# A fused two-block kernel on one core: attentions with a deeper order, six weight places, norms split by bank

## The reference

```python
# first block
h = rms_norm(x, norm_mix);  u = h @ w_in                  # 4896 columns
y_a = short_conv(u);  y_n = nsa_mixer(u);  y_g = gated_deltanet(u)
x = x + (sum_r sigmoid(h @ w_gate + b_gate)_r * (y_r @ w_branch[r])) @ w_out
h = rms_norm(x, norm_ffn)
x = x + hier_moe(h)        # 4 groups x 8 = 32 experts, the best group, 2 experts in it, FF 512
# second block: modulate(t, shift, scale) comes from silu(c) @ ada_w
x = x + g1 * mla_mixer(modulate(rmsnorm(x)));   x = x + g2 * swiglu(modulate(rmsnorm(x)))
x = x + g1 * mamba2_mixer(modulate(rmsnorm(x))); x = x + g2 * moe_swiglu(modulate(rmsnorm(x)))
return rmsnorm(x, final_norm)                             # moe_swiglu: 8 experts
```

## Time and profile before

| | us |
|---|---|
| median of 3 runs | 2620.92 |
| lowest and highest | 2620.5, 2622.52 |
| the profiled execution | 2633.1 |
| its span in the trace | 2631.3 |
| PE busy in it | 2230.7 (85%) |
| DVE busy | 1436.3 (55%) |
| ACT busy | 1155.0 (44%) |
| mean granted clock of PE | 0.894 |

### The profile page before, as it was taken

The page is one execution under the profiler, slowest core; times in us unless marked ns, Lnnn a source line. Parts: engine busy times, 40 slices in busy tenths (PEclk is TensorE's granted clock), DMA queues, the critical chain, the costliest instruction groups (busy, mean ns, idle before and its releaser), DMA issues.

```text
span 2631.3 us, 29041 instructions
## 1 busy us (share of the span) xinstructions
PE 2230.7 (85%) x11922; PEld 1662.9 (63%) x11922; DVE 1436.3 (55%) x1992; ACT 1155.0 (44%) x1489; POOL 40.9 (2%) x107
## 2 busy tenths in 40 slices
PE   6888898766677665787799889888999999999997
PEld 6767566552222211455799777667887888878875
DVE  4744435333011000332455576557989988988997
ACT  3432333320000000242344356645777777777775
POOL 0000100000000000000000000000000000000000
PEclk9889898767777788897899889788999999999999
DMA  7451830219999999657344432134989989989994
GB/s 255 167 185 49 281 135 33 96 64 387 409 409 409 409 409 409 248 198 287 112 156 182 160 128 97 64 128 158 343 319 370 336 321 369 338 318 372 337 341 193
DMA packets 267688, 656.66 MB, mean 250 GB/s; under 512 B 13454, under 2 KB 38546, under 8 KB 267544
## 3 DMA queue, kind: packets, MB, share of 16 engines
q1 hardware_dynamic: 266592, 652.90, 67.1%
q10 hardware_dynamic: 952, 1.77, 0.2%
HBM read 653.60 MB, written 1.05 MB: 249 GB/s over the span
## 4 chain that ended last, share of the span: by engine, by line
PE 67%; DMA 16%; DVE 9%; ACT 5%; issue 2%; POOL 0%; ACTq 0%; DVEq 0%; POOLq 0%
PE psum L241 16%; PE psum L242 16%; PE psum L243 16%; PE psum L236 11%; DMA ring<-in_w_expert_up 5%; DMA ring<-in_w_expert_down 5%; DMA ring<-in_w_expert_gate 5%; PE psum L2278 2%; PE psum L1043 2%; DVE w_lo L186 2%; PE psum L835 1%; ACT w_hi L176 1%; PE psum L2300 1%; DVE xbc L841 1%; DMA ring<-in_ada_w 1%
## 5 line engine op out<-in xcount | busy, mean ns | idle before, releaser
L186 DVE TENSOR_TENSOR w_lo<-ring,w_hi 128x1024 fp32r<-128x1024 f32 (+1 forms) x778 | 904.8, 1179 | 404.0 <-ACT w_hi L176 391.0
L176 ACT CAST w_hi<-ring 128x1024 fp32r<-128x1024 f32 (+1 forms) x778 | 785.2, 1015 | 448.5 <-PE psum L243 444.9
L241 PE MATMUL psum<-w_hi,xg_hi 128*128 128x512 f32 (+1 forms) x768 | 293.9, 383 | 1.2 <-ACT xg_lo L1961 1.2
L243 PE MATMUL psum<-w_lo,xg_hi 128*128 128x512 f32 (+1 forms) x768 | 288.8, 376 | 0.0
L242 PE MATMUL psum<-w_hi,xg_lo 128*128 128x512 f32 (+1 forms) x768 | 288.7, 376 | 0.0
L2278 PE MATMUL psum<-ring,hT 128*32 128x512 f32 x1024 | 169.8, 799 | 117.3 <-DMA ring<-in_w_expert_gate 62.7
L2278 PEld LDWEIGHTS psum<-ring,hT 128*32 128x32 f32 x1024 | 32.6, 129 | 248.7 <-DMA ring<-in_w_expert_up 86.6
L241 PEld LDWEIGHTS psum<-w_hi,xg_hi 128*128 128x128 f32 x768 | 144.6, 188 | 30.5 <-issue 1.8
L242 PEld LDWEIGHTS psum<-w_hi,xg_lo 128*128 128x128 f32 x768 | 144.6, 188 | 29.0 <-issue 1.7
L243 PEld LDWEIGHTS psum<-w_lo,xg_hi 128*128 128x128 f32 x768 | 144.4, 188 | 28.5
L2130 DVE TENSOR_TENSOR x<-x,psum 128x1024 f32<-128x1024 f32 x14 | 17.1, 1221 | 244.0 <-PE psum L236 244.0
(11 more groups left out here) (653 smaller groups left out, 3838.0 us busy)
## 6 DMA issues: line engine op xcount, KB each, us to landing
ring<-in_moe_w_gate SPq DMA_DIRECT2D x40, 2048.0 KB, 9.4
ring<-in_moe_w_up SPq DMA_DIRECT2D x40, 2048.0 KB, 10.2
ring<-in_moe_w_down SPq DMA_DIRECT2D x40, 2048.0 KB, 9.2
ring<-in_w_expert_gate SPq DMA_DIRECT2D x32, 2048.0 KB, 16.7
ring<-in_w_expert_up SPq DMA_DIRECT2D x32, 2048.0 KB, 17.1
ring<-in_w_expert_down SPq DMA_DIRECT2D x32, 2048.0 KB, 17.7
ring<-in_ada_w SPq DMA_DIRECT2D x24, 2048.0 KB, 8.3
ring<-in_ssm_w_in SPq DMA_DIRECT2D x10, 2048.0 KB, 8.0
```

What stands on the lines that cost most here:

```text
L176: a.copy(self.buffers(n, src.shape)[0], src).then_inc(*self.hi_made.up())
L186: v.tensor_tensor(lo, src, hi.bitcast(F32), SUB).then_inc(*self.lo_made.up())
L241: p.matmul(o, l[0], r[0], start=start, stop=False)
L243: return p.matmul(o, l[0], r[1], start=False, stop=stop)
```

## The change

1. **Attentions.** PE multiplies the values of job m-1 behind the transposes of job m; before it did those of job m right behind its own transposes. DVE's `finish` comes one step later too. The loops have one more step, in which `beside` isn't called.
2. **Places.** Six of the twelve units of group 0 have buffers of their own: gate 0 and 1 in memory of the NSA mixer (`place_ns`), up 2 and 3 in memory of `w_hi` and `w_lo` (`place_w`), down 0 and 1 in memory of the stage's own tensors (`place_fe`). SP waits for the end of the NSA mixer before the first two and for the last multiplied unit of the output projection before the other four.
3. **Table.** `table_dve` is cut in five pieces of three rounds, one in each of the groups 1 to 5, behind the gather.
4. **Norms.** Of each bank pair DVE turns tiles 0 and 1 and ACT tiles 2 and 3 into `hT`; the high and low halves are made by two tiles, and PE starts on the first four tiles and waits for the others at its fifth (`ready`). The router's logits take tiles 0 to 3 for both token tiles first. The state space mixer's `dt` product waits for `hT` alone.
5. **Weights of the groups.** The reciprocal and two multiplications that weight the gates by the group's probability stand behind the start of the places' count.

The diff, cut to its core:

```diff
@@ Ring @@
+    def add_beside(self, src, tensor, loaded):
+        self.beside.append((src, tensor, loaded))
+        return -len(self.beside)
+    def load_beside(self, e, u):
+        src, tensor, loaded = self.beside[-u - 1]
+        src = src(None)
+        e.dma_start(tensor[:, :].rearrange("p (k n) -> p k n", k=src.shape[1]), src).then_inc(loaded, 16)
@@ memory @@
+    place_w = [sb(f"place_w{n}", [P, UNIT], where=places) for n in range(2)]
+    sb("under_places", [P, 1248], where=mg)
+    place_ns = [sb(f"place_ns{n}", [P, UNIT], where=mg) for n in range(2)]
+    place_fe = [sb(f"place_fe{n}", [P, UNIT], where=fe) for n in range(2)]
+    places = {(0, 0, 0): place_ns[0], (0, 0, 1): place_ns[1], (0, 1, 2): place_w[0], (0, 1, 3): place_w[1], (0, 2, 0): place_fe[0],
+              (0, 2, 1): place_fe[1]}
@@ norm_dve @@
-            for k in range(4):
+            for k in range(2):
...
-        if h is not None:
-            for k4 in (0, 4):
-                v.wait_ge(*st.act.of("h_hi", k4))
-                v.tensor_tensor(h[1][:, k4:k4 + 4, :], hT[:, k4:k4 + 4, :], h[0][:, k4:k4 + 4, :].bitcast(F32),
-                                SUB).then_inc(*st.dve.up("h", k4))
+            if h is not None:
+                for k in ((0, 2) if k4 == 0 else (2, 0)):
+                    two = slice(k4 + k, k4 + k + 2)
+                    v.wait_ge(*st.act.of("h_hi", k4 + k))
+                    v.tensor_tensor(h[1][:, two, :], hT[:, two, :], h[0][:, two, :].bitcast(F32), SUB).then_inc(*st.dve.up("h", k4))
@@ ACT's part of a norm @@
-    def norm_split_act(a, st, h):
+    def norm_turned_act(a, st, h, gain, shift):
         for k4 in (0, 4):
-            a.wait_ge(*st.dve.of("hT", k4))
-            a.copy(h[0][:, k4:k4 + 4, :], hT[:, k4:k4 + 4, :]).then_inc(*st.act.up("h_hi", k4))
+            a.wait_ge(*st.pe.of("hT", k4))
+            ps = banks.of(st.name, "hT", k4)
+            for k in (2, 3):
+                a.activation(hT[:, k4 + k, :], ps[:, k * T:(k + 1) * T], ACT.Identity if shift else ACT.Copy, scale=gain(k4 + k),
+                             bias=shift(k4 + k) if shift else 0.0).then_inc(*st.act.up("hT", k4))
+            banks.empty(st.act, st.name, "hT", k4)
+            if h is not None:
+                for k in ((0, 2) if k4 == 0 else (2, 0)):
+                    a.wait_ge(*(st.act if k else st.dve).of("hT", k4))
+                    a.copy(h[0][:, k4 + k:k4 + k + 2, :], hT[:, k4 + k:k4 + k + 2, :]).then_inc(*st.act.up("h_hi", k4 + k))
@@ by_feature_pe; by_token_pe likewise @@
+                if ready and f == 0 and k == 4:
+                    p.wait_ge(*ready)
@@ attention_pe @@
-        for n in range(len(jobs) + AHEAD):
+        for n in range(len(jobs) + AHEAD + 1):
...
-            if beside:
+            if beside and n < len(jobs) + AHEAD:
                 beside(p, n)
             m = n - AHEAD
-            if m >= 0:
+            if 0 <= m < len(jobs):
...
                 ins.then_inc(*st.pe.up("shown", m))
+            m -= 1
+            if m >= 0:
+                job = jobs[m]
                 p.wait_ge(*st.act.of("pT", m))
                 ps = banks.take(p, st.name, "out", m)
@@ attention_dve @@
-            m = n - AHEAD
+            m = n - AHEAD - 1
@@ logits @@
+    def logits_pe(p, st, w):
+        ps = banks.take(p, st.name, "logits")
+        for k4 in (0, 4):
+            for signal in (st.dve, st.act):
+                p.wait_ge(*signal.of("hT", k4))
+            for t in range(NT):
+                for k in range(k4, k4 + 4):
+                    ins = p.matmul(ps[:, t * 512:t * 512 + w.shape[2]], hT[:, k, t * P:(t + 1) * P], w[:, k, :],
+                                   start=k == 0, stop=k == KD - 1)
@@ groups_dve @@
-                table_dve(v, S["moe1"], moe1)
...
+            if 1 <= i < 6:
+                table_dve(v, S["moe1"], moe1, 3 * (i - 1), MOST_OVER_GROUPED if i == 5 else 3 * i)
@@ mix_act @@
         split.make_hi(a, PARTS)
...
-        norm_split_act(a, st, h_mix)
+        norm_turned_act(a, st, h_mix, lambda k: col("norm_mix", k), None)
@@ sync @@
         start_sync(s)
+        ring.load(s, run1.units[0, 0, 2])
+        finished(s, S["nsa"])
+        for n in range(2):
+            ring.load_beside(s, run1.units[0, 0, n])
+        ring.load(s, run1.units[0, 1, 1] + 1)
+        s.wait_ge(*split.multiplied(unit["out", 1]))
+        for g, n in ((1, 2), (1, 3), (2, 0), (2, 1)):
+            ring.load_beside(s, run1.units[0, g, n])
         ring.load(s, run1.units[31 // GROUP, 2, 3] + 1)
```

More of the change, by code:

```diff
@@ L110, in __init__ @@
         self.units, self.emptied, self.now, self.next = [], None, {}, 0
+        self.beside = []
     def restart(self):
@@ L131, in loaded @@
     def loaded(self, u):
+        if u < 0:
+            return self.beside[-u - 1][2], 16
         return self.slot_loaded[u % SLOTS], 16 * (u // SLOTS + 1)
     def slot(self, u):
+        if u < 0:
+            return self.beside[-u - 1][1][:, :]
         return self.tensor[:, u % SLOTS, :]
     def empty(self, signal, u):
-        self.now[u] = signal.last()
+        if u >= 0:
+            self.now[u] = signal.last()
 class Split:
@@ L804, in by_token_pe @@
             kn = hi.shape[1]
+            if ready and k0 == 4:
+                p.wait_ge(*ready)
             for half, out_ in enumerate(outs):
@@ L951, in mix_pe @@
         norm_pe(p, st, xn_mix)
-        for k4 in (0, 4):
-            p.wait_ge(*st.dve.of("h", k4))
+        p.wait_ge(*st.dve.of("h", 0))
         for n in range(3):
-            by_feature_pe(p, unit["conv", n], h_mix)
+            by_feature_pe(p, unit["conv", n], h_mix, ready=None if n else st.dve.of("h", 4))
         for n in range(4):
@@ L2436, in moe1_pe @@
         norm_pe(p, st, xn_ffn)
-        p.wait_ge(*st.dve.of("hT", 4))
-        ps = banks.take(p, "moe1", "logits")
-        for t in range(NT):
-            ins = product(p, ps[:, t * 512:t * 512 + 36], [(hT[:, k, t * P:(t + 1) * P], w_rout[:, k, 0:36]) for k in range(KD)])
-        ins.then_inc(*st.pe.up("logits"))
+        logits_pe(p, st, w_rout[:, :, 0:36])
         places_pe(p, st, moe1)
@@ L2563, in mla_pe @@
             ps = banks.take(p, "unit", u)
-            by_token_pe(p, u, h_mla, [[ps[:, t * 512:t * 512 + w] for t in range(NT)]])
+            by_token_pe(p, u, h_mla, [[ps[:, t * 512:t * 512 + w] for t in range(NT)]], ready=None if n else st.dve.of("h", 4))
         modulation_pe(p, st, spread0)
@@ L2845, in ffn_pe @@
         norm_pe(p, st, xn_ff)
-        for k4 in (0, 4):
-            p.wait_ge(*st.dve.of("h", k4))
+        p.wait_ge(*st.dve.of("h", 0))
         for c, nf in enumerate(ff_chunks):
             for g in range(2):
-                by_feature_pe(p, unit["ff", g, c], h_ff, nf)
+                by_feature_pe(p, unit["ff", g, c], h_ff, nf, ready=None if c or g else st.dve.of("h", 4))
         pairs = [banks.take(p, "ff_down", half) for half in range(2)]
@@ L2972, in ssm_pe @@
         ins.then_inc(*e.up("dt"))
-        by_feature_pe(p, unit["ssm", "b", 0], h_ssm)
+        p.wait_ge(*st.dve.of("h", 0))
+        by_feature_pe(p, unit["ssm", "b", 0], h_ssm, ready=st.dve.of("h", 4))
         modulation_pe(p, st, spread1)
@@ L3356, in moe2_pe @@
         norm_pe(p, st, xn_moe)
-        p.wait_ge(*st.dve.of("hT", 4))
-        ps = banks.take(p, "moe2", "logits")
-        for t in range(NT):
-            ins = product(p, ps[:, t * 512:t * 512 + 8], [(hT[:, k, t * P:(t + 1) * P], w_rout[:, k, 36:44]) for k in range(KD)])
-        ins.then_inc(*st.pe.up("logits"))
+        logits_pe(p, st, w_rout[:, :, 36:44])
         for t in range(NT):
```

61 lines of the change are left out of this document (38 added, 23 removed).

## The result

| | us | ratio to before |
|---|---|---|
| kernel before, median | 2620.8 | |
| changed kernel, median of 4 (2527.8 to 2540.1) | 2536.0 | 0.9671 [0.9645, 0.9697] |
| changed kernel, a later set, median of 5 (2538.0 to 2542.8) | 2542.1 | 0.9689 [0.9675, 0.9702] |
| profiled execution of the changed kernel | span 2526.1, run 2527.8 | |

It is 85 us faster in the first set and 79 in the later one, where 66 were forecast; the first lies at the lower end of the range. Executions of one kernel differ: by 12 us here, and the kernel before lay between 2616.2 and 2633.1 in all of its runs. The profiled execution of the changed kernel is the fastest of its four, while the profiled one of before was 12 us above its median. The two traces are therefore 105 us apart and the medians 85.

What follows compares the result with a forecast made beforehand. No single bound: the chain is 67% PE and 16% DMA, so each part was weighed where it lies. The terms -25.7 - 11 - 13.4 - 12.0 - 4 = -66.1 took the median 2620.92 to 2555 us, range 2536 to 2578.

Steps and rivals of the forecast that it cites:

- Places, -25.7: First experts' groups: six units leave the DMA traffic, 30.7 us, less 3.5 for a later first slot and 1.5 empty queue.
- NSA attention, -11: NSA attention: most of PE's 17.7 us of waits for ACT's copies of the turned probabilities go, saving 11 us.
- rival D: Both attentions: waits move to bank pairs or DVE's scaling, some 15 of 24.4 us come back; 2570 us, chance 0.12.
- MLA attention, -13.4: MLA attention: six waits of about 1.07 us go (6.4), and PE ends 7.0 us earlier at the last job.
- Norms, -12.0: Six norms: DVE and ACT share the tiles, so PE starts earlier in five; first norm 1.0 us longer; sum -12.0.
- The three small steps: First experts' norm: three small DVE steps leave the path, saving 0.75 us.
- Clock, -4: NSA attention: denser work regains a quarter of the clock loss in two low stretches, 4 us, bounds 0 and 14.
- Rival B: Both attentions: the clock stays at 2.4 GHz, 10 us more gained; 2545 us, chance 0.16.
- A: Whole kernel: the sum of the terms holds; 2555 us, own range 2542 to 2568, chance 0.55.
- C: First experts' group 0 doesn't keep up, by half clock or an empty queue; places give -16, 2565 us, chance 0.14.
- E: Both attentions: transposes and products side by side bring PE to half clock; slower, 2674 us, chance 0.03.
- The sum: Whole kernel: the five terms together give -66.1 us, from the median of 2620.92 to 2555.

Runs made afterwards that it cites:

- e3_norms: The kernel before with the norms by banks and the moved weights of the groups alone: 2604.0 us, ratio 0.9936.
- e8_norm_filler: The changed kernel with 20 to 24 unread identity products on PE ahead of the transposes of four norms: 2533.1 us, ratio 0.9662.
- after_again: The changed kernel as it is, measured once more in a later set: 2542.1 us, ratio 0.9689.

## Why the prediction came out too high

**Places, -25.7.** Right: 25.8 in the stage, 23.8 alone. The 5.12 us for a unit, the first slot 3.5 us later and the ten units in time held; the 1.5 us of an empty queue did not occur. The trace keeps 409 GB/s, so the figure of 358 GB/s in the Trainium skill, "DMA: Bandwidth & Descriptors", section "Where 436 GB/s comes from", doesn't bind here. The table in pieces cost nothing, as counted. Whole it takes 10.6 us of the stage, less than half of the 22 us of small steps that the prediction put there. In nine traces with the six places and the table in pieces the stage takes 454.0 to 455.0 us, whatever the clock.

**NSA attention, -11.** Right as a term for the waits: 11.5. The two waits for banks came, but longer (5.4 with 2.8 foreseen). Of the 15 us of rival D, at 0.12, these 5.4 are all that came.

**MLA attention, -13.4.** Too much for its mechanism: 9.8. The term is more than PE waited for the copies there at all, 12.3: its 7.0 for the end stand against waits of 4.81 and 1.10. The end of the earlier trace rows is shorter as meant, the last transposes lie in the wait and both products follow each other, but that wait is still 2.5 us, because ACT's four high halves of the output weights stand ahead of the copy as before.

**Norms, -12.0.** The five norms were forecast at -1.75, -3.2, -3.1, -2.2 and -2.0 and gave -2.0, -3.2, -3.1, -2.2 and -2.3; the first norm +1.0 and gave +0.7. The three small steps, forecast at -0.75, gave -0.9 (logits to the selection 14.47 and, in e3_norms, 13.55). The heading says -14, but the sum goes by -12.0. Beside them 3.2 us in the last experts were not foreseen. Part alone: 16.5.

**Clock, -4.** This is the step that failed. It was read from two stretches of the NSA attention alone, a quarter of their 14.5 us, nothing for MLA and nothing behind the norms. Removing the waits raised the clock in both attentions and was worth about 12 us for the order alone (33.1 less 21.3 of waits) and 14 to 21 in the changed kernel (35.6 to 42.4 less 21.3). Rival B named the mechanism and had 0.16, but was priced from the same two stretches, 10 us more than A, so that even it ended at 2545. The reason given against it, the first experts at 0.77 with PE busy two thirds of the time, was no argument: that stage is full of gaps (one of 2 to 3 us for each unit), and its clock rose from 0.78 to 0.88 in the trace after without any gain: e8_norm_filler has 0.78 in it and takes only 1.0 us more, since DMA sets its end. The rule of the Trainium skill, "TensorE: Matmul & The Clock Gate", section "What's actually happening", that activity releases the throttle, would have given the better number; fillers that change nothing but PE's activity show it in this kernel, though the stretch from 390.9 us on, at 0.51 with PE busy throughout, fits it less well.

**Rivals C and E** did not come: no wait for DMA in group 0, and no half clock through the attentions.

**The sum.** Alone, the parts save 23.8, 33.1 and 16.5 us, 73.4 together, with 25.7, 28.4 (order and clock) and 12.0 forecast. So 7.3 of what was missed lies in the order and the norms, where the clock gave 8 more than its 4 and the MLA term 3.6 less than was counted. The other 6 to 11 us, up to 79.4 or 84.8, are seen only with the parts together; what makes them stays open.

A second fault lies under the sum: the terms were taken from one trace, 12 us above the median, in which the NSA attention was at the slow one of its two values (150.0 against 143.4).

## What to carry to other kernels

In a stage like these attentions, where PE has most of the work and waits a microsecond or more in each step, count its gaps twice: once as waits, and once for the half clock that they leave behind; here the second was half to all of the first (12 to 21 us for 21.3). In a wait that can't be removed, products that nobody reads can be worth more than they cost, if they have their bank at once and end before the wait does, and if work of PE's own follows and not the next wait. Units loaded ahead of a stage that DMA bounds count in full, but only while no other engine's small work stands in the group that now runs through.

## What the runs showed of the hardware

- PE's granted clock went to half behind waits of quite different length: in the trace after, products took 0.63 us instead of 0.39 for some 6 us behind a wait of 1.69 us at 398.31, and in after_again the clock was 0.50 over 16.5 us behind one of 3.52. In the trace before it was 0.51 over 17 us with no wait above 1.2 us in the 17 us ahead.
- It also went to 0.51 for 3.5 us with no wait above 0.7 us in the 40 us ahead (390.90 in the trace after).
- The same gap in the same program was followed by half clock in one execution and not in another: the MLA attention of the changed kernel took 94.5 or 88.5 us, and the executions of one kernel in one set spread over 2 to 15 us.
- Products of the identity, 128x128 in float32, were issued in 0.23 us each at full clock (14 in 3.29 us) and in 0.37 partly at half (20 in 7.44).
- Ahead of group 0, four loads of 2 MB, issued from 524.14 on, ran beside the norm without delaying it: it took 3.44 us, as in e3_norms without these loads.
- Over the 454 us of the first experts' groups a granted clock of 0.78 or 0.88 made no difference of more than 1.0 us (e8_norm_filler and after), with DMA at 409 GB/s.
